# A recurrent loop's start-up moved among the last two column tiles of the projection before it

## The chip, the cores and the metric

The kernel runs on one core of a Trainium2 chip. One launch computes two transformer-like blocks in fp32; the time is the device time of one execution, in microseconds (us). A core has five engines that run their own instruction streams side by side and meet only at semaphores: TensorE (PE, matmuls), VectorE (DVE), ScalarE (ACT, activation functions), GpSimd (POOL) and SyncE (SP, which issues the transfers).

## The reference, cut to what matters

The second block mixes tokens in two ways; the part touched here is the RWKV mixer. 768 tokens (256 of context, 512 of the sequence) are projected to r, k, v and three small latents, each passed through a three-tap convolution over tokens. Then, for 8 heads of 64 and for two directions, a decay rate, a gain and a recurrence are computed:

```
parts = h @ p['w_in'];  rw = dwconv(parts[..., :RWKV_COLS], p['rwkv_conv'])
r, k, v, wl, al, gl = jnp.split(rw, RWKV_SPLITS, axis=-1)
kk = heads(k * p['k_k']);  kk = kk / jnp.maximum(norm(kk), 1e-12)
w_lat = jnp.tanh(wl)
for each direction:
    w = -softplus(-(w0 + w_lat @ w2)) - 0.5;  decay = exp(-exp(w))
    a = sigmoid(a0 + al @ a2)
    k_dir = k * (1.0 + (a - 1.0) * p['k_a'])
step: sa = einsum('bhvk,bhk->bhv', S, kk_t)
      S  = S * w_t - sa * b_t + v_t * k_t        # b = kk * a
      y  = einsum('bhvk,bhk->bhv', S, r_t)
```

## The kernel before, in words

The program is a list of phases. In a phase each engine has a function of its own, and `build` runs them in order; at the end of a phase every engine drains, raises its `phase_end` semaphore and waits until all the others have raised theirs (`boundary`, L615 on). If a phase is marked `soft`, TensorE alone doesn't wait there; it goes on into the next phase, and a call of `settle` (L516) later makes it wait for the other engines' `phase_end`.

**The projection** (`rwkv_projection`, L2469) works through 14 `items`: the two latent groups, then four column tiles each of k, r and v (`items[10]` to `items[13]` are the v tiles). For a k or v tile TensorE runs 8 matmuls of 256 columns (the context tokens) and 8 of 512 columns (the sequence), all by `block_feature` (L512), into one of three pairs of PSUM banks, `pair(n) = n % 3` (banks 0 to 5). ScalarE then copies both parts with the middle tap (L2594), and VectorE adds the two neighbour taps (L2619, L2621, twice each). `free` counts tiles that VectorE has finished, so it tells when a pair of banks may be written again. Banks 6 and 7 serve the norm of kk and the bonus term; the last to use them are the bonus sums of item 11 (L2572), copied out by ScalarE (L2614, counted by `bonus_copied`). `floored` counts the four normalised kk tiles (last written at L2657). ScalarE ends the phase by touching the sigmoid table with a one-element activation (L2615).

**The loop** (`rwkv_loop`, L2684) handles 12 chunks of 64 tokens in both directions. Two chunks make a block. For a block, in each direction `d`: `latents(b, d)` is one matmul of 512 columns and four of 128 on 33 rows (L2747, L2749) into banks 2 and 3; `rate(b, d)` is two sigmoids on ScalarE (L2942, L2943), to `SIG` and `RATE`; `cums(b, d)` sums the rates over tokens with 8 small matmuls (L2758; 16 in the profile, since an fp32 matmul is recorded as two) into banks 2 and 3; `exps(b, d)` is three activations with the exponential (L2950, L2951, L2954; a fourth in blocks of the sequence); `rate_products` and `key_products` are six VectorE operations (L3012, L3016, L3022) and `products(b, d)` three for a context block (L3030, L3034, L3036). For block 0 this is the loop's prologue: nothing overlaps it, and bank pair 2, 3 is written four times in turn. For later blocks the same helpers are called between the steps of earlier chunks.

The chunk loop then starts at n = -1 with `gram(0, B)` (L2680, 16 matmuls of a 64x64 tile, into bank 6), `latents(1, 0)`, `gram(0, K)` (L2673), `latents(1, 1)`, and from n = 0 on goes through five levels per chunk (`t_level`, `xy_level`: matmuls of 64x64 tiles, with copies on ScalarE at L2970 and, on VectorE, a subtraction at L3058 and a transposition at L3042 between them). At n = -1 VectorE's part is: mask gram B (L3047, `evacuate_b`), make Y (L3039, `y_init`), mask gram K (L3053), transpose (L3042). GpSimd adds the identity to Y (L3130, `eye`) and masks the level matrices (L3121); it has nothing to do in the projection. The order of the work is the order in which the code is written; there is no planner here.

`RW` places the loop's tiles in three areas of on-chip memory that are free once the loop runs: the projection's scratch (`R_TMP` on), its input (`A_A`), and the ring of weight tiles (`O_RING`), which the projection reads until its last matmul.

Of the kernel before, what the change touches and what calls it, by code (L numbers as in the profile page):

```python
# [20 lines left out]
P = 128  # L21
D = 1024
KD = D // P
S = 512
# [1995 lines left out]
for _n, _w in (("x1", 2 * CH), ("y1", 2 * CH), ("gram", 8 * CH), ("level", LEVELS * 2 * CH), ("eye", CH),  # L2020
# [8 lines left out]

RW = regions([(R_TMP, WORDS), (A_A, A_B), (O_RING, O_VEC)],  # L2030
             [("AR", 4096), ("X", 2048), ("B", 2048), ("K", 2048), ("GB", 2048), ("GK", 2048), ("LOFF", LEVELS * 512),
              ("SIG", 1024), ("RATE", 1024), ("VTK", 1024), ("S", 1024), ("T", 512), ("KTK", 512), ("BTK", 512), ("KV", 512),
              ("SA", 512)])
# [435 lines left out]
def rwkv_projection(k):  # L2469
# [60 lines left out]

    def tensor(k, pe):
        for n, (x, f) in enumerate(items):
            if n < 2:
                continue
            if n % 2 == 0:
                wt = k.pe_stream.take(KD, 256)
            if n >= 3:
                pe.wait_ge(free, n - 2)
            else:
                pe.wait_ge(k.attention["spread_read"], k.attention_count["spread_read"] + 2)  # L2540
            two = [k.bank[2 * pair(n)], k.bank[2 * pair(n) + 1]]
            _, _, m, c0 = part(n)
            if x in "kv":
                block_feature(pe, two[1][0:m, :NC_CTX], wt, c0, m, lambda q: C[:, q, :], KD)
            block_feature(pe, two[0][0:m, :], wt, c0, m, lambda q: A[:, q, :], KD).then_inc(k.half_done, 1)
            if n == 2:
                settle(k, pe, "diff_post")
            if x == "k":
                if f == 0:
                    pe.wait_ge(k.rwkv_in, 16 * N_RWKV_LOADS)  # L2550
                    pe.wait_ge(free, 1)
                else:
                    pe.wait_ge(gained, 2 * f)
                for d in range(2):
                    pe.matmul(k.bank[6 + d], W2A[64:97, d, f * P:(f + 1) * P], WA[64:97, NC_CTX:], start=True,
                              stop=True).then_inc(gains, 1)
            if x == "r":
                if f == 0:
                    pe.wait_ge(gained, 8)
                else:  # L2560
                    pe.wait_ge(rooted, f)
                pe.wait_ge(squared, f + 1)
                pe.matmul(k.bank[6], HEADSUM, SQ[:, f % 2, 0:512], start=True, stop=True)
                pe.matmul(k.bank[7][:, :256], HEADSUM, SQ[:, f % 2, 512:768], start=True, stop=True).then_inc(summed, 1)
            if x == "v" and f < 2:
                for g in (2 * f, 2 * f + 1):
                    pe.wait_ge(weighed, g + 1)
                    if f == 0:
                        pe.wait_ge(rooted, 4)
                    else:  # L2570
                        pe.wait_ge(bonus_copied, g - 1)
                    pe.matmul(k.bank[6 + g % 2], HEADSUM, BT[:, g, :], start=True, stop=True).then_inc(bonus_sum, 1)  # L2572

    def scalar(k, act):
        for n, (x, f) in enumerate(items):
            if x == "r":
# [40 lines left out]
    def vector(k, dve):  # L2617
        def neighbours(x, y, taps, cnt):
# [10 lines left out]
        for n, (x, f) in enumerate(items):  # L2629
            dve.wait_ge(centred, n + 1)  # L2630
# [28 lines left out]
    return Phase("rwkv_projection", sync=sync, tensor=tensor, vector=vector, scalar=scalar)  # L2659
# [24 lines left out]
def rwkv_loop(k):  # L2684
# [50 lines left out]

    halves = lambda n, lv, d: 2 * LEVELS * n + 2 * lv + d + 1
# [5 lines left out]
    def tensor(k, pe):  # L2742
        wait = lambda name, value: pe.wait_ge(sems[name], value)

        def latents(b, d):
            tok = block_tokens(b, d)
            pe.matmul(k.bank[2], WA[0:33, tok], W2A[0:33, d, :], start=True, stop=True)  # L2747
            for f in range(4):
                mm = pe.matmul(k.bank[3][:, f * P:(f + 1) * P], W2A[64:97, d, f * P:(f + 1) * P], WA[64:97, tok],  # L2749
# [3 lines left out]
        def cums(b, d):  # L2753
            wait("rated", prep(b, 1))
            sums = mask(k, "sums", 0, 256).rearrange("p (w c t) -> p w c t", w=2, c=2)
            for f in range(4):
                for c, rows in enumerate(HEADS):
                    mm = pe.matmul(k.bank[2 + c][:, f * P:(f + 1) * P], SIG[d][rows, f * P:(f + 1) * P], sums[rows, :, c, :],  # L2758
# [135 lines left out]
        pe.wait_ge(k.rwkv_in, 16 * N_RWKV_LOADS)  # L2894
        latents(0, 0)
        wait("rated", 1)
        latents(0, 1)
        wait("rated", 2)
        cums(0, 0)
        wait("exps", 1)  # L2900
        cums(0, 1)
        for n in range(-1, NCH + 1):
            m, g, live = n - 1, n + 1, 0 <= n < NCH
            for lv in range(LEVELS):
# [13 lines left out]
                if lv == 1:  # L2918
# [3 lines left out]
                    else:  # L2922
                        rest(aside)
                if lv in (3, 4) and rated_in(n) is not None:
                    prepare(n, lv - 3)
# [11 lines left out]
    def scalar(k, act):  # L2937
        wait = lambda name, value: act.wait_ge(sems[name], value)

        def rate(b, d):  # L2940
            wait("latent_done", prep(b, d))
            act.activation(SIG[d], k.bank[2], ACT.Sigmoid)  # L2942
            act.activation(RATE[d], k.bank[3], ACT.Sigmoid).then_inc(sems["rated"], 1)  # L2943

        def exps(b, d):
            wait("cums_done", prep(b, d))
            cum = k.psum[:, 1024:2048].rearrange("p (c f w t) -> p f w c t", c=2, f=4, w=2)
# [12 lines left out]
        for d in range(2):  # L2960
            rate(0, d)
        for d in range(2):
            exps(0, d)
        for n in range(-1, NCH + 1):
# [31 lines left out]
    def vector(k, dve):  # L2996
# [76 lines left out]
        dve.memset(ST[0], 0.0).then_inc(sems["state"], 1)  # L3073
        rate_products(0)
        key_products(0)
        for d in range(2):
            products(0, d)
        for n in range(-1, NCH + 1):
# [59 lines left out]
    return Phase("rwkv_loop", tensor=tensor, vector=vector, scalar=scalar, pool=pool)  # L3138
# [289 lines left out]
```

## Time and profile before

| | us |
|---|---|
| median of 3 runs | 2642.1 (2641.81 to 2643.7) |
| the profiled execution: its own time | 2645.46 |
| its span, from the first to the last instruction | 2643.7 |
| TensorE busy | 2487.0 (94% of the span) |
| VectorE, ScalarE, GpSimd busy | 1346.0, 513.4, 127.6 |
| projection's last two v tiles on TensorE | 1767.67 to 1788.32 |
| loop's prologue | 1788.32 to 1807.38 |
| chunk loop | 1807.38 to 2119.9 |

The span is one profiled execution. Instructions have a start and a duration; an engine's idle time is put down to the semaphore event that ended it. The chain of waits follows the work that ended last back from the end, so what lies on it sets the time. "PEclk" is the TensorE clock that was granted: 1.00 is 2.4 GHz and 0.50 is 1.2 GHz.

### The profile page before, as it was taken

How to read it: one execution, taken by the hardware profiler on the slowest of the kernel's cores; microseconds unless marked ns; L12 is line 12 of the kernel's file. 1: busy time of each engine (PE TensorE's matmuls, PEld its weight loads, DVE VectorE, ACT ScalarE, POOL GpSimd, SP SyncE). 2: the span in 40 equal slices, each digit the busy share in tenths (PEclk: the TensorE clock that was granted, in tenths of full speed). 3: DMA queues.
4: the chain of work that ended last, by engine and by line, in shares of the span. 5: the costliest groups of instructions: out<-in, count | busy, mean ns of one | idle time of the engine just before them, and what ended most of it. 6: DMA issues, size and time to landing. Idle time of an engine off the chain costs nothing.

```text
span 2643.7 us, 45304 instructions
## 1 busy us (share of the span) xinstructions
PE 2487.0 (94%) x19512; PEld 1932.5 (73%) x19512; DVE 1346.0 (51%) x2582; ACT 513.4 (19%) x1032; POOL 127.6 (5%) x106
## 2 busy tenths in 40 slices
PE   8989999999999999999998999997888898999997
PEld 5945888888586548888885664556788846888786
DVE  5625555533454426555432255465666536787533
ACT  2122100100003421000001034223434222212100
POOL 0000000000000000000000000002322200000000
PEclk9988999999999999999999989997999998999998
DMA  5323322233212014222234200300000033223232
GB/s 167 122 78 128 96 67 93 76 88 108 65 65 65 1 64 128 66 94 86 66 88 144 69 32 15 104 0 2 4 4 4 4 103 121 78 83 96 53 86 69
DMA packets 221166, 190.28 MB, mean 72 GB/s; under 512 B 8727, under 2 KB 219064, under 8 KB 220968
## 3 DMA queue, kind: packets, MB, share of 16 engines
q1 hardware_dynamic: 220674, 187.29, 22.9%
q8 instruction: 155, 2.54, 0.4%
q14 instruction: 43, 0.35, 0.0%
q10 hardware_dynamic: 294, 0.09, 0.0%
HBM read 185.25 MB, written 2.10 MB: 71 GB/s over the span
## 4 chain that ended last, share of the span: by engine, by line
PE 87%; DVE 6%; ACT 2%; issue 2%; SPq 1%; DMA 1%; POOL 1%; DVEq 0%; POOLq 0%; ACTq 0%
PE psum L1630 30%; PE psum L1840 14%; PE psum L512 8%; PE psum L2673 6%; PE psum L1130 4%; PE psum L1344 3%; PE psum L1341 3%; PE psum L3211 2%; PE psum L542 2%; PE psum L2680 1%; PE psum L1066 1%; PE psum L2252 1%; PE psum L2270 1%; PE psum L1109 1%; DVE sbuf L3042 1%
## 5 line engine op out<-in xcount | busy, mean ns | idle before, releaser
L1630 PE MATMUL psum<-sbuf 128*128 128x256 f32 x3696 | 804.5, 381 | 3.5 <-DVE sbuf L476 1.9
L1630 PEld LDWEIGHTS psum<-sbuf 128*128 128x128 f32 x3696 | 705.9, 191 | 101.7 <-issue 3.1
L1840 PE MATMUL psum<-sbuf 128*128 128x256 f32 x1848 | 405.2, 382 | 11.1 <-DVE sbuf L1858 5.5
L1840 PEld LDWEIGHTS psum<-sbuf 128*128 128x128 f32 x1848 | 353.8, 192 | 62.1 <-DVE sbuf L1858 6.3
L1714 DVE TENSOR_TENSOR sbuf<-sbuf,psum 128x256 f32<-128x256 f32 x462 | 177.8, 417 | 200.0 <-PE psum L1630 198.7
L512 PE MATMUL psum<-sbuf 128*128 128x512 f32 (+3 forms) x688 | 247.9, 519 | 4.3 <-DVEq L617 4.0
L2673 PE MATMUL psum<-sbuf 64*64 64x64 f32 (+1 forms) x5952 | 209.6, 223 | 32.4 <-DVE sbuf L3058 10.1
L2673 PEld LDWEIGHTS psum<-sbuf 64*64 64x64 f32 x5952 | 194.8, 136 | 44.5 <-issue 24.5
L512 PEld LDWEIGHTS psum<-sbuf 128*128 128x128 f32 (+2 forms) x688 | 129.4, 189 | 115.5 <-issue 103.4
L1876 DVE TENSOR_TENSOR sbuf<-sbuf,psum 128x256 f32<-128x256 f32 x84 | 34.2, 419 | 231.6 <-PE psum L1840 231.2
L427 POOL TENSOR_TENSOR sbuf<-sbuf 128x512 f32<-128x512 f32 x30 | 37.8, 1279 | 1923.1 <-DVE sbuf L413 1922.9
L1130 PE MATMUL psum<-sbuf 128*128 128x512 f32 x256 | 117.0, 607 | 0.0
L1650 ACT ACTIVATE sbuf<-sbuf 128x512 f32<-128x512 f32 x44 | 27.7, 630 | 399.7 <-DVE sbuf L1714 399.7
L3121 POOL TENSOR_TENSOR sbuf<-sbuf 128x512 f32<-128x512 f32 x60 | 75.0, 1273 | 576.1 <-DVE sbuf L3047 545.7
L1130 PEld LDWEIGHTS psum<-sbuf 128*128 128x128 f32 x256 | 48.1, 195 | 53.1 <-issue 53.1
L1700 DVE TENSOR_TENSOR sbuf<-sbuf 128x512 f32<-128x512 f32 x66 | 44.5, 690 | 81.1 <-PE psum L1630 67.1
L1344 PE MATMUL psum<-sbuf 128*128 128x256 f32 x392 | 85.4, 379 | 0.0
L1344 PEld LDWEIGHTS psum<-sbuf 128*128 128x128 f32 x392 | 74.2, 190 | 11.3 <-issue 1.3
L1178 DVE TENSOR_REDUCE sbuf<-psum 128x1 f32<-128x256 f32 (+3 forms) x80 | 36.8, 460 | 89.1 <-PE psum L1066 51.7
L3058 DVE TENSOR_TENSOR sbuf<-sbuf,psum 128x256 f32<-128x256 f32 x120 | 47.6, 403 | 66.5 <-PE psum L2673 66.1
L1341 PEld LDWEIGHTS psum<-sbuf 128*128 128x128 f32 x672 | 75.4, 192 | 0.1
L1341 PE MATMUL psum<-sbuf 128*128 128x128 f32 x672 | 75.4, 275 | 0.0
(281 smaller groups left out, 2687.9 us busy)
## 6 DMA issues: line engine op xcount, KB each, us to landing
sbuf<-in_w_mod_dram SPq DMA_DIRECT2D x24, 1024.0 KB, 5.1
sbuf<-in_w_ffn_gate_dram SPq DMA_DIRECT2D x22, 1024.0 KB, 5.5
sbuf<-in_w_ffn_up_dram SPq DMA_DIRECT2D x22, 1024.0 KB, 8.0
sbuf<-in_w_ffn_down_dram SPq DMA_DIRECT2D x32, 704.0 KB, 6.0
sbuf<-in_w_up_dram SPq DMA_DIRECT2D x22, 1024.0 KB, 7.2
sbuf<-in_w_out_dram SPq DMA_DIRECT2D x12, 1024.0 KB, 7.7
sbuf<-in_w_in_dram SPq DMA_DIRECT2D x12, 1024.0 KB, 5.5
sbuf<-in_w_down_dram SPq DMA_DIRECT2D x16, 704.0 KB, 5.8
```

Source lines behind the costliest of these rows:

```text
L512: mm = pe.matmul(bank, w[:, q, c0:c0 + m], rhs(k0 + q), start=start and q == 0, stop=stop and q == kc - 1)
L542: mm = pe.matmul(bank, act_chunk(q), w[:, q, :], start=q == 0, stop=q == kc - 1)
L1130: mm = pe.matmul(bank_of(b), tiles[b // 2][:, q, (b % 2) * P:(b % 2) * P + P], MIX[:, q, :], start=q == 0, stop=q == KD - 1)
L1341: mm = pe.matmul(self.bank(p)[:, t * P:(t + 1) * P], x[:, q, t * P:(t + 1) * P], w[:, q, :], start=q == 0, stop=q == 3)
L1344: mm = pe.matmul(self.bank(p), w[:, q, :], x[:, q, :], start=q == 0, stop=q == 3)
L1630: mm = pe.matmul(bank, w[:, q, :], rhs[:, q, :], start=q == 0, stop=q == 3)
L1714: dve.tensor_tensor(out, base, bank_of(u, p, t), ALU.add).then_inc(s["added"], 1)
L1840: mm = pe.matmul(bank_of(g, p), wt[:, q, :], rhs_of[p][:, q, :], start=q == 0, stop=q == UNITS - 1)
L2673: mm = pe.matmul(out[h], lhsT[h], rhs[h], start=start, stop=stop)
L3058: dve.tensor_tensor(y, y, k.bank[d][:, 256:512], ALU.subtract).then_inc(sems["xy"], 1)
L3121: pool.tensor_tensor(split(LOFF[lv]), split(GB[g % 2][:, :, 0, :]), both_level(lv), ALU.mult).then_inc(sems["loff"], 1)
L3211: mm = pe.matmul(block_bank(b), tiles[b // 2][:, q, (b % 2) * P:(b % 2 + 1) * P], MIX[:, q, :], start=q == order(b)[0], stop=q == order(b) ...
```

## The change

Each engine's function of the loop becomes a generator (`tensor_steps`, `scalar_steps`, `vector_steps`) with `yield` between the parts of the prologue. The projection's functions start these generators and take their steps at set places among items 12 and 13; the loop's own phase runs what remains. The prologue's banks for block 0 come from `home`: 6 and 7 for direction 0, 4 and 5 for direction 1. The projection is marked soft, and TensorE settles after `gram(0, B)`, before `latents(1, 0)`. Loop tiles that block 0 writes this early are placed elsewhere (`RW_RING`).

```diff
+RW_RING = [("RATE", 1024), ("B", 2048), ("LOFF", LEVELS * 512), ("K", 2048), ("VTK", 1024), ("S", 1024), ("T", 512), ("KTK", 512), ("BTK", 512), ("KV", 512), ("SA", 512)]
...
+    def begin(k, name, eng):
+        steps = k.rwkv_steps[name] = k.rwkv_steps[name](k, eng)
+        next(steps)
+        return steps
     def tensor(k, pe):
+        steps = begin(k, "tensor", pe)
...
+            if n == 13:
+                pe.wait_ge(free, 12)
+                next(steps)
             if x in "kv":
                 block_feature(pe, two[1][0:m, :NC_CTX], wt, c0, m, lambda q: C[:, q, :], KD)
+            if n == 12:
+                pe.wait_ge(bonus_copied, 4)
+                next(steps)
+            if n == 13:
+                next(steps)
             block_feature(pe, two[0][0:m, :], wt, c0, m, lambda q: A[:, q, :], KD).then_inc(k.half_done, 1)
...
     def scalar(k, act):
+        steps = begin(k, "scalar", act)
         for n, (x, f) in enumerate(items):
+            if n == 12:
+                act.activation(k.M[0:1, O_SML + 205:O_SML + 206], k.eps[0:1, :], ACT.Sigmoid)
+                next(steps)
+            if n == 13:
+                act.wait_ge(floored, 4)
+                next(steps)
...
     def vector(k, dve):
+        steps = begin(k, "vector", dve)
...
         for n, (x, f) in enumerate(items):
+            if n == 13:
+                dve.wait_ge(floored, 4)
+                next(steps)
             dve.wait_ge(centred, n + 1)
...
-    return Phase("rwkv_projection", sync=sync, tensor=tensor, vector=vector, scalar=scalar)
+    ph = Phase("rwkv_projection", sync=sync, tensor=tensor, vector=vector, scalar=scalar)
+    ph.soft = True
+    return ph
...
+    home = lambda b, d: 2 if b else (6, 4)[d]
...
-    def tensor(k, pe):
+    def tensor_steps(k, pe):
...
-        pe.wait_ge(k.rwkv_in, 16 * N_RWKV_LOADS)
+        yield
         latents(0, 0)
-        wait("rated", 1)
+        yield
         latents(0, 1)
-        wait("rated", 2)
-        cums(0, 0)
-        wait("exps", 1)
-        cums(0, 1)
+        yield
+        for d in range(2):
+            cums(0, d)
+        yield
         for n in range(-1, NCH + 1):
...
+                if n == -1 and lv == 3:
+                    settle(k, pe, "rwkv_projection")
                 if lv in (3, 4) and rated_in(n) is not None:
                     prepare(n, lv - 3)
...
-    def scalar(k, act):
+    def scalar_steps(k, act):
...
-        for d in range(2):
-            rate(0, d)
+        yield
+        rate(0, 0)
+        yield
+        rate(0, 1)
         for d in range(2):
             exps(0, d)
+        yield
...
-    def vector(k, dve):
+    def vector_steps(k, dve):
...
-        dve.memset(ST[0], 0.0).then_inc(sems["state"], 1)
+        yield
         rate_products(0)
         key_products(0)
         for d in range(2):
             products(0, d)
+        yield
+        dve.memset(ST[0], 0.0).then_inc(sems["state"], 1)
         for n in range(-1, NCH + 1):
```

On TensorE, before the change, items 11 to 13 are followed by the prologue and by gram B (L512 is the projection, L2747 and L2749 the latents, L2758 the sums, L2680 gram B, L2673 gram K):

```order
L2572 MATMUL psum<-sbuf 128x512 x2
L512 MATMUL psum<-sbuf 128x256 x8
L512 MATMUL psum<-sbuf 128x512 x8
L512 MATMUL psum<-sbuf 128x256 x8
L512 MATMUL psum<-sbuf 128x512 x8
L2747 MATMUL psum<-sbuf 128x512
L2749 MATMUL psum<-sbuf 128x128 x4
L2747 MATMUL psum<-sbuf 128x512
L2749 MATMUL psum<-sbuf 128x128 x4
L2758 MATMUL psum<-sbuf 128x128 x16
L2680 MATMUL psum<-sbuf 64x64 x16
```

And with the change, in the same stretch of TensorE (the latents are now L2775 and L2777, the sums L2786, gram B L2707):

```order
L2585 MATMUL psum<-sbuf 128x512 x2
L512 MATMUL psum<-sbuf 128x256 x8
L2775 MATMUL psum<-sbuf 128x512
L2777 MATMUL psum<-sbuf 128x128 x4
L512 MATMUL psum<-sbuf 128x512 x8
L2775 MATMUL psum<-sbuf 128x512
L2777 MATMUL psum<-sbuf 128x128 x4
L512 MATMUL psum<-sbuf 128x256 x8
L2786 MATMUL psum<-sbuf 128x128 x16
L512 MATMUL psum<-sbuf 128x512 x8
L2707 MATMUL psum<-sbuf 64x64 x16
```

The latents stand before the sequence part of item 12 and before the context part of item 13; both directions' sums stand between the two parts of item 13; gram B follows the last projection matmul directly.

On VectorE, with the change, this stands around items 12 and 13 (L2641 and L2643 are the neighbour taps, L3046 to L3070 the prologue's products, L3113 the clearing of the state, L3081 the masking of gram B):

```order
L2643 SCALAR_TENSOR_TENSOR sbuf<-psum,sbuf 128x255
L3046 SCALAR_TENSOR_TENSOR sbuf<-sbuf 128x512 x2
L3050 TENSOR_TENSOR sbuf<-sbuf 128x512 x2
L3056 SCALAR_TENSOR_TENSOR sbuf<-sbuf 128x512 x2
L3064 TENSOR_TENSOR sbuf<-sbuf 128x8x64
L3068 TENSOR_TENSOR sbuf<-sbuf 128x512
L3070 TENSOR_TENSOR sbuf<-sbuf 128x512
L3064 TENSOR_TENSOR sbuf<-sbuf 128x8x64
L3068 TENSOR_TENSOR sbuf<-sbuf 128x512
L3070 TENSOR_TENSOR sbuf<-sbuf 128x512
L2641 SCALAR_TENSOR_TENSOR sbuf<-psum,sbuf 128x511
L2643 SCALAR_TENSOR_TENSOR sbuf<-psum,sbuf 128x511
```

All twelve product operations now stand between the taps of item 12 and the taps of item 13; before, they stood after item 13's taps and the clearing of the state.

On ScalarE the same stretch, with the change (L2614 is the middle tap, L2972 and L2973 the rates, L2981 to L2985 the exponentials):

```order
L2973 ACTIVATE sbuf<-psum 128x512
L2981 ACT_TABLE_LOAD
L2981 ACTIVATE sbuf<-psum 128x8x64
L2982 ACTIVATE sbuf<-psum 128x512
L2985 ACTIVATE sbuf<-psum 128x8
L2981 ACTIVATE sbuf<-psum 128x8x64
L2982 ACTIVATE sbuf<-psum 128x512
L2985 ACTIVATE sbuf<-psum 128x8
L2614 ACTIVATE sbuf<-psum,sbuf 128x512
L2614 ACTIVATE sbuf<-psum,sbuf 128x256
L2635 ACT_TABLE_LOAD
L2635 ACTIVATE sbuf<-sbuf 1x1
```

The rates and exponentials of block 0 now stand ahead of item 13's middle tap, and the load of the sigmoid table, three loads in all as before, is the last thing of the phase.

## Rows read from the trace of the kernel before

**Rows 1.** The page: granted clock in 40 slices of the span, and the chain by engine.
```profile
PEclk9988999999999999999999989997999998999998
...
PE 87%; DVE 6%; ACT 2%; issue 2%; SPq 1%; DMA 1%; POOL 1%; DVEq 0%; POOLq 0%; ACTq 0%
```

**Rows 2.** Chain of waits, 1735 to 1835 us: start, us on the chain, engine and line.
```profile
1767.67 20.65 PE psum L512 x64
...
1798.67 2.10 PE psum L2758 x16
...
1807.38 1.97 PE psum L2680 x32
...
1811.36 1.90 PE psum L2673 x32
...
1815.27 2.78 PE psum L2673 x48
...
1823.16 0.68 PE psum L2673 x16
...
1826.10 0.33 PE psum L2673 x4
...
1828.64 1.09 PE psum L2758 x16
```

**Rows 3.** Busy time by stage: stretch, length, PE, PEld, DVE, ACT, POOL, PEclk, DMA, GB/s.
```profile
1767.67:1788.32 20.65, 20.64 (x64) 11.81 (x63) 4.15 (x8) 1.65 (x3) 0.00 (x0) 1.00 0.00 1
1788.32:1807.38 19.06, 8.22 (x52) 7.07 (x52) 10.62 (x17) 9.59 (x16) 0.00 (x0) 0.60 0.00 0
1792.12:1819.40 27.28, 19.85 (x206) 17.86 (x208) 12.23 (x23) 9.90 (x18) 7.40 (x6) 0.50 0.00 1
1819.40:2119.90 300.50, 259.18 (x8688) 244.78 (x8685) 183.06 (x396) 115.28 (x247) 82.22 (x66) 1.00 0.02 4
```

**Rows 4.** Chain of waits, 1850 to 1865 us: latents of a later block.
```profile
1854.57 0.31 PE psum L2747
...
1855.66 0.64 PE psum L2673 x16
```

**Rows 5.** Timeline, all engines, 1788 to 1813 us: start, us, engine, line; in brackets idle before.
```profile
1788.35 1.05 ACT L2594 ACTIVATE sbuf<-psum,sbuf 128x512 f32<-128x512 f32 x2 [9.27 <-PE psum L512]
1789.42 1.28 ACT L2615 ACT_TABLE_LOAD   x1
1790.71 0.20 ACT L2615 ACTIVATE sbuf<-sbuf 1x1 f32<-1x1 f32 x1
...
1791.98 1.11 PE L2747 MATMUL psum<-sbuf 33*128 33x512 f32 x1 [3.67 <-DVEq L617]
...
1792.25 0.48 DVE L3073 MEMSET sbuf<- 128x512 f32 x1 [0.37 <-issue]
...
1797.44 0.60 ACT L2942 ACTIVATE sbuf<-psum 128x512 f32<-128x512 f32 x1 [2.23 <-PE psum L2749]
...
1800.37 1.29 DVE L3022 SCALAR_TENSOR_TENSOR sbuf<-sbuf 128x512 f32<-128x512 f32 x2
...
1805.31 0.69 DVE L3030 TENSOR_TENSOR sbuf<-sbuf 128x512 f32<-128x512 f32 x1 [1.31 <-ACT sbuf L2954]
...
1809.40 0.69 DVE L3047 TENSOR_TENSOR sbuf<-psum,sbuf 128x512 f32<-128x512 f32 x1 [2.08 <-PE psum L2680]
1810.01 0.68 DVE L3039 TENSOR_TENSOR sbuf<-psum,sbuf 128x512 f32<-128x512 f32 x1
1811.49 1.27 POOL L3130 TENSOR_TENSOR sbuf<-sbuf 128x512 f32<-128x512 f32 x1
```

**Rows 6.** Timeline of PE at two places: an earlier phase, and the second level.
```profile
903.91 1.25 PE L1094 MATMUL psum<-sbuf 128*128 128x128 f32 x8 [2.16 <-ACT sbuf L1245]
...
1819.12 1.44 PE L2673 MATMUL psum<-sbuf 64*64 64x64 f32 x32 [0.24 <-DVE sbuf L3042]
```

**Rows 7.** Busy time just behind the first row of rows 6; columns as in rows 3.
```profile
905.00:908.00 3.00, 3.00 (x5) 0.97 (x4) 0.80 (x2) 0.18 (x1) 0.00 (x0) 0.50 0.00 0
```

More of the change, by code:

```diff
@@ L2027 @@
 assert R_G2 + 512 <= A_MIX
+RW_RING = [("RATE", 1024), ("B", 2048), ("LOFF", LEVELS * 512), ("K", 2048), ("VTK", 1024), ("S", 1024), ("T", 512), ("KTK", 512), ("BTK", 512), ("KV", 512), ("SA", 512)]
 RW = regions([(R_TMP, WORDS), (A_A, A_B), (O_RING, O_VEC)],
-             [("AR", 4096), ("X", 2048), ("B", 2048), ("K", 2048), ("GB", 2048), ("GK", 2048), ("LOFF", LEVELS * 512),
-              ("SIG", 1024), ("RATE", 1024), ("VTK", 1024), ("S", 1024), ("T", 512), ("KTK", 512), ("BTK", 512), ("KV", 512),
-              ("SA", 512)])
+             [("AR", 4096), ("X", 2048), ("GB", 2048), ("GK", 2048), ("SIG", 1024)] + RW_RING)
 MOD_DERIVED = ("gx", "gc", "gf", "pm", "pf")
@@ L2746, in latents @@
             tok = block_tokens(b, d)
-            pe.matmul(k.bank[2], WA[0:33, tok], W2A[0:33, d, :], start=True, stop=True)
+            pe.matmul(k.bank[home(b, d)], WA[0:33, tok], W2A[0:33, d, :], start=True, stop=True)
             for f in range(4):
-                mm = pe.matmul(k.bank[3][:, f * P:(f + 1) * P], W2A[64:97, d, f * P:(f + 1) * P], WA[64:97, tok],
+                mm = pe.matmul(k.bank[home(b, d) + 1][:, f * P:(f + 1) * P], W2A[64:97, d, f * P:(f + 1) * P], WA[64:97, tok],
                                start=True, stop=True)
@@ L2757, in cums @@
                 for c, rows in enumerate(HEADS):
-                    mm = pe.matmul(k.bank[2 + c][:, f * P:(f + 1) * P], SIG[d][rows, f * P:(f + 1) * P], sums[rows, :, c, :],
+                    mm = pe.matmul(k.bank[home(b, d) + c][:, f * P:(f + 1) * P], SIG[d][rows, f * P:(f + 1) * P], sums[rows, :, c, :],
                                    start=True, stop=True)
@@ L2941, in rate @@
             wait("latent_done", prep(b, d))
-            act.activation(SIG[d], k.bank[2], ACT.Sigmoid)
-            act.activation(RATE[d], k.bank[3], ACT.Sigmoid).then_inc(sems["rated"], 1)
+            act.activation(SIG[d], k.bank[home(b, d)], ACT.Sigmoid)
+            act.activation(RATE[d], k.bank[home(b, d) + 1], ACT.Sigmoid).then_inc(sems["rated"], 1)
         def exps(b, d):
             wait("cums_done", prep(b, d))
-            cum = k.psum[:, 1024:2048].rearrange("p (c f w t) -> p f w c t", c=2, f=4, w=2)
+            o = 512 * home(b, d)
+            cum = k.psum[:, o:o + 1024].rearrange("p (c f w t) -> p f w c t", c=2, f=4, w=2)
             incl, excl = cum[:, :, 0], cum[:, :, 1]
@@ L3136, in pool, with remaining, steps @@
                     loff(g, lv)
-    return Phase("rwkv_loop", tensor=tensor, vector=vector, scalar=scalar, pool=pool)
+    k.rwkv_steps = {"tensor": tensor_steps, "scalar": scalar_steps, "vector": vector_steps}
+    def remaining(name):
+        def steps(k, eng):
+            for _ in k.rwkv_steps[name]:
+                pass
+        return steps
+    return Phase("rwkv_loop", tensor=remaining("tensor"), vector=remaining("vector"), scalar=remaining("scalar"), pool=pool)
 def mixer_output(k, w, post):
```

## The prediction

> **What bounds the kernel now.** I read the page first: TensorE is the chain for 87% of the span, and its granted clock is near full everywhere but in some slices, the lowest of them (7 tenths) being the one that holds the start of the chunk loop [rows 1]. Then the table by stage. Over the last two v tiles TensorE is busy for 20.64 of 20.65 us at a clock of 1.00; in the prologue it is busy for 8.22 of 19.06 us, VectorE for 10.62 and ScalarE for 9.59, and none of these shares is near one: the stage is a relay in which each engine waits for the one before [rows 3]. The chain of waits says the same: TensorE is done with the projection at 1788.32 (1767.67 + 20.65), and gram B begins at 1807.38 [rows 2]. These 19.06 us are what the change can touch. The clock falls in them: from 1792.12 to 1819.40 it is 0.50, that is 1.2 instead of 2.4 GHz, and in the rest of the loop 1.00 [rows 3].
>
> **The work that TensorE takes into the projection.** Latents for two directions and sums for two directions. At full clock one direction's latents take 1.09 us (from 1854.57 to the next piece at 1855.66) [rows 4], and one direction's sums 1.09 us, against 2.10 in the prologue at half clock [rows 2]. Among the tiles TensorE has the full clock [rows 3], so the price is 4 x 1.09 = 4.36 us, and the last projection matmul ends at 1788.32 + 4.36 = 1792.68. Bounds: 4.36 at full clock; at half clock about 8.4.
>
> **Is everything in time among the tiles?** An item takes 20.65 / 2 = 10.32 us, a third of it (3.44) for the context columns, the rest 6.88. So latents 0 run at 1771.11 to 1772.20, and ScalarE, which is idle there (1.65 us busy in the whole stretch [rows 3]), has the table and both sigmoids done long before the sequence part ends at 1779.1. Latents 1 run to 1780.2. ScalarE's queue holds item 12's taps first (1.05 us, to 1780.2) and then the rates (two of 0.60 us, to 1781.4) [rows 5]; the exponential's table, 1.28 us, follows, to 1782.7. TensorE's context part ends at 1783.6, so the sums, which wait for the second rate, find it done 2.2 us before. They run to 1784.7 and 1785.8; the exponentials of direction 1 are done about 1787.1. VectorE finishes item 12's taps about 1782.7, then six rate and key products at 1.2 to 1.3 us for each two [rows 5], to 1786.3, and three products for each direction at about 2.05 us (the last three began at 1805.31 and gram B at 1807.38, rows 5 and 2), to 1790.4. Gram B needs them at 1792.68. The cover is 2.3 us. If it were gone, every us beyond it would be one on the path, but only on the way to gram B, which itself is not late before the tail below ends; the true slack is larger.
>
> **What is late next: the tail of item 13.** Its taps can't move. Before, the other engines were past the phase's end, and TensorE with them, at 1791.98, 3.66 us after the last matmul, and VectorE's clearing of the state began at 1792.25, 3.93 us after it [rows 5]. With the soft boundary TensorE runs gram B in that time for nothing, at about 1 us. VectorE's clearing then starts at 1792.68 + 3.93 = 1796.61 and, 0.48 us later, the masking of gram B at 1797.09. Before it began at 1809.40 [rows 5]: 12.3 us earlier. The new wait, settle, stands before latents 1, 0 on TensorE; behind it are gram K and all levels. It ends at 1792.68 + 3.66 = 1796.34; the latents take 1.09 us at full clock or 2.00 at half (between gram B's end, 1809.35, and 1811.36 [rows 2]), so at most to 1798.35. Y is ready 1.29 us after the masking begins (1810.01 + 0.68 - 1809.40 [rows 5]): 1798.38. So gram K starts at about 1798.4 in either case, where it started at 1811.36 [rows 2]: **12.96 us earlier**.
>
> A page of the Trainium skill speaks against this tail: ScalarE: Activation LUTs, section What ACT_TABLE_LOAD costs, gives about 2.66 us for every switch of table, a load of 1283 ns and a drain of about 1380 ns. The trace has the load at 1.28 us, and the activation behind it starts at 1790.71, at once [rows 5]; no drain is seen. With the page's drain ScalarE would end its phase at about 1792.3 instead of 1790.9, in the times of before, 0.3 us after the 1791.98 at which the phase ended, and the gain would be 12.6 instead of 12.96; I go by the row.
>
> **From gram K on: two levels of clock.** After gram B TensorE is idle from about 1793.7 to 1796.34, 2.6 us, then has 1 or 2 us of latents on 33 rows, an idle stretch of up to 1 us, gram K, and latents again. In an earlier phase an idle time of 2.16 us, ended at 903.91, was followed by a clock of 0.50 from 905 on [rows 6, 7]. In the loop the clock holds at 1.00 [rows 3]. I take it that the clock falls again. Then gram K (1.90), the latents behind it and the first level go as before: level 0 begins 3.91 us after gram K (1815.27 - 1811.36 [rows 2]) and level 1 3.85 us after that (1819.12 [rows 6]). The clock came back 4.1 us after level 0 began (1819.40 [rows 3]); if it now comes a few us later, that costs up to 0.9. If the clock doesn't fall, gram K takes 1 us less, but level 0 then waits for GpSimd's identity, done 3.36 us after the masking (1811.49 + 1.27 - 1809.40 [rows 5]), at 1800.45, and a transposition: it begins near 1801.0, 14.3 us earlier than before, and a level takes 2.94 us (1826.10 - 1823.16 [rows 2]) instead of 3.85: together 15.2 us earlier.
>
> **Further edits.** The new places of tiles, the generators and the banks of block 0 add no instruction but one table touch, under ScalarE's idle time. No transfer moves: SP's next loads wait for the loop's end, before and after. What follows level 1 is the same chain in the same order, so I count it at nothing; where a later pause makes the clock fall a little sooner or later, 1 or 2 us either way.
>
> **The sum.** -12.96, and 0.1 for the later return of the clock: -12.9. Against the profiled execution's own time, 2645.46, that is 2632.6; this execution is 3.4 above the median of the runs shown, 2642.1, and against that it is **2629.2**.
>
> **Rival A: the clock never falls.** For it: the idle time falls from over 10 us in pieces to one of 2.6. Against it: 2.16 us have sufficed elsewhere. Gain 15.2: 2626.9.
>
> **Rival B: a wait inside the projection.** TensorE takes up to three hand-overs among the tiles (bonus copies, the freed bank pair, the rates), each of which my times cover with 1 to 3 us. If one of the in-order queues is later than I think, or if the masking waits for VectorE longer than the tail, 3 to 5 us come back; in the prologue at half clock this work took about 8.4 us of TensorE instead of 4.36, a loss of the same size. Gain 8 to 10: about 2633. Against it: the work on ScalarE and VectorE in this stretch was 1.65 and 4.15 of 20.65 us [rows 3], so even with the prologue's shares neither is full.
>
> **Rival C, slower: the half clock stays in the loop.** The gap now lies right before the loop, whose levels are bursts of 64x64 matmuls with pauses. If these did not lift the clock, each level would cost 3.85 instead of 2.94 us, 0.91 more. The gain of 12.9 is used up after 14 levels, close to three of the 12 chunks; through half of the 60 levels it would be 27.3 - 12.9 = 14 us slower, 2656, and through all of them 42, 2684. Against it: the same levels lifted it before, within 4.1 us of their start.
>
> **Rival D: nothing changes**, 2642.1, if the soft boundary only moved the relay. It would take item 13's tail to be as long as the prologue; it is 3.93 of 19.06 us.
>
> **How the numbers follow.** The forecast with the clock fallen 0.56, A 0.20, B 0.16, C 0.04, D 0.04. A run of this kernel can tell 0.2%, 5.3 us, from no change. Forecast, A and B lie beyond it on the fast side, together 0.92; with the part of D and C that ends near zero: faster 0.93, same 0.04, slower 0.03. The range takes A with 1.5 us for a clock that falls differently elsewhere, 2625.4, and B's upper middle, 2634.2; what is outside is B's worst, C and D, and part of A, under 0.2.
>
> **What the new profile would show.** Right: the two v tiles' stretch on TensorE without a pause, 4.4 us longer, at a clock of 1.00; latents and sums at 1.09 us each; twelve products on VectorE before item 13's taps; gram B directly behind the last projection matmul; then one wait of about 2.6 us on TensorE, ended by VectorE; from the projection's old end to the masking of gram B 8.8 us instead of 21.1. A low clock that begins three to seven us after gram B and ends within the first two levels. Wrong: a pause on TensorE before the sums, or before gram B for the products (rival B); a clock of 1.00 throughout (A); a slice of the loop at half clock (C); a chunk loop, from gram B's masking on, longer than before by more than 1 us.

## The result and the profile after

The changed kernel takes 2629.85 us (median of 6 runs, 2625.46 to 2633.36), the kernel before 2641.95 on the same chip (6 runs, 2636.23 to 2643.7). The medians lie 12.1 us apart, where 12.9 and a time of 2629.2 had been forecast. The ratio on record, with its 95% interval, is 0.9947 (0.9932 to 0.9963). It isn't the quotient of the two medians, which is 0.9954; it stands for 14.0 us, and its interval for 9.8 to 18.0, so the change is faster beyond the noise and its size is known to a few us only. The profiled execution of the changed kernel took 2627.17 us with a span of 2625.4, and that of before had 2645.46 and 2643.7. So the two profiles lie 18.3 us apart and the medians 12.1. Both numbers have to be explained.

The page, as in [rows 1]: the slice that holds the start of the loop no longer stands out.

```profile
PEclk9988999999999999999999989999999998999998
```

The chain of waits of the changed kernel, which answers to [rows 2]: start, us on the chain, engine and line.

```profile
1767.86 3.45 PE psum L512 x16
...
1772.40 7.06 PE psum L512 x16
...
1780.56 3.65 PE psum L512 x16
1784.21 1.99 PE psum L2786 x32
1786.19 7.08 PE psum L512 x16
...
1793.30 0.69 ACT sbuf L2614
...
1797.19 0.48 DVE sbuf L3113
...
1798.87 1.97 PE psum L2700 x32
...
1802.85 2.78 PE psum L2700 x48
...
1806.70 1.81 PE psum L2700 x32
...
1810.99 0.68 PE psum L2700 x16
```

Busy time by stage as in [rows 3], in the same columns: the last two v tiles, the tail, the stretch at half clock, and the rest of the loop.

```profile
1767.67:1792.68 25.01, 25.01 (x117) 15.55 (x115) 11.73 (x20) 8.84 (x17) 0.00 (x0) 1.00 0.00 1
1792.60:1797.00 4.40, 1.88 (x36) 1.10 (x34) 2.37 (x4) 2.54 (x4) 0.00 (x0) 1.00 0.00 0
1797.95:1808.19 10.24, 9.22 (x137) 8.58 (x136) 4.77 (x12) 3.19 (x7) 7.42 (x6) 0.50 0.01 2
...
1813.00:2107.00 294.00, 258.71 (x8558) 242.18 (x8557) 179.66 (x391) 117.38 (x249) 82.17 (x66) 1.00 0.03 9
```

TensorE is busy through the whole of the two tiles (25.01 of 25.01 us), also with the prologue's work in it, and VectorE and ScalarE do theirs beside it (11.73 and 8.84 us, where [rows 3] had 4.15 and 1.65). The relay of 19.06 us has shrunk to the tail of item 13. The stretch at half clock is 10.24 us long instead of 27.28.

The timelines of ScalarE, VectorE and TensorE over the same place, which answer to [rows 5].

```profile
1781.79 1.28 ACT L2981 ACT_TABLE_LOAD   x1
1785.35 0.60 ACT L2981 ACTIVATE sbuf<-psum 128x512 f32<-128x512 f32 x1 [2.28 <-PE psum L2786]
...
1794.36 1.28 ACT L2635 ACT_TABLE_LOAD   x1
1795.66 0.20 ACT L2635 ACTIVATE sbuf<-sbuf 1x1 f32<-1x1 f32 x1
```

```profile
1789.81 0.69 DVE L3070 TENSOR_TENSOR sbuf<-sbuf 128x512 f32<-128x512 f32 x1
1794.38 0.75 DVE L2641 SCALAR_TENSOR_TENSOR sbuf<-psum,sbuf 128x511 f32<-128x511 f32 x1 [3.88 <-ACT sbuf L2614]
...
1797.60 0.63 DVE L3081 TENSOR_TENSOR sbuf<-psum,sbuf 128x512 f32<-128x512 f32 x1
```

```profile
1793.36 1.15 PE L2707 MATMUL psum<-sbuf 64*64 64x64 f32 x32
1796.92 0.69 PE L2775 MATMUL psum<-sbuf 33*128 33x512 f32 x1 [2.41 <-DVEq L617]
...
1798.87 1.97 PE L2700 MATMUL psum<-sbuf 64*64 64x64 f32 x32 [0.78 <-DVE sbuf L3073]
```

All twelve products end at 1790.50, and gram B stands directly behind the last projection matmul. TensorE's long wait behind it, 2.41 us, is ended by the phase's end; a short one of 0.78 us stands before gram K.

**Where the 18.3 us of the two profiles lie.** At the second level (1806.70 against 1819.12 [rows 6]) the changed kernel is 12.42 us ahead. The next phase begins at 2119.92 before and at 2101.28 after, 18.64 us apart; so another 6.22 us lie inside the chunk loop, whose code the change leaves as it is (what follows the loop gives 0.3 back). Three chains of waits, at the first matmuls of that phase: before, the changed kernel, and the changed kernel in a second profiled execution (the run "again" below).

```profile
2119.92 2.84 PE psum L3179 x6
```

```profile
2101.28 2.84 PE psum L3223 x6
```

```profile
2112.12 2.84 PE psum L3223 x6
```

From the second level to this row it is 300.80 us before, 294.58 in the first profile of the changed kernel, and 303.95 (from 1808.17) in its second. The same program differs from itself by 9.4 us there. The chains show where: in pieces of "issue", such as these of the changed kernel's first profile, and in the run "again" in two further spells at half clock.

```profile
1847.00 1.30 issue
...
1918.10 1.41 issue
```

Over this stretch "issue" has 6.2% of the chain before (18.6 us), 4.7% in the first profile of the changed kernel (13.8) and 6.1% in its second (18.5): 4.8 of the 6.22 us, and 4.7 of the 9.4. The profiles of the other runs below have 295 to 300 us for the same stretch (fill 296.9, hard 297.4, head 300.4, head_fill 295.2, twice 297.8, products_back 295.8, rates_only 299.6), in no order that follows their edits. So I count the 12.4 us that stand at the second level as the change's, and the 6.2 us behind it as chance of one execution. The medians (12.1) agree; their interval is too wide to exclude a small effect inside the loop.

### The profile page after: what moved, and what is told of

Same layout as the page of the kernel before. It is cut to its first block, busy times and chain, and to the rows that moved or that the text cites. A ratio compares the mean times of both kernels' runs of the same rounds, so it can differ in the third digit from the quotient of the medians.

```text
span 2625.4 us, 45306 instructions
## 1 busy us (share of the span) xinstructions
PE 2481.6 (95%) x19512; PEld 1930.4 (74%) x19512; DVE 1344.9 (51%) x2582; ACT 513.1 (20%) x1033; POOL 127.6 (5%) x106
## 4 chain that ended last, share of the span: by engine, by line
PE 87%; DVE 6%; ACT 2%; issue 1%; SPq 1%; POOL 1%; DMA 1%; DVEq 0%; POOLq 0%; ACTq 0%
PE psum L1630 31%; PE psum L1840 15%; PE psum L512 8%; PE psum L2700 6%; PE psum L1130 4%; PE psum L1344 3%; PE psum L1341 3%; PE psum L3255 2%; PE psum L542 2%; PE psum L1066 1%; PE psum L2251 1%; PE psum L2707 1%; PE psum L2269 1%; PE psum L1109 1%; PE psum L325 1%
## 5 line engine op out<-in xcount | busy, mean ns | idle before, releaser
L512 PE MATMUL psum<-sbuf 128*128 128x512 f32 (+3 forms) x688 | 250.0, 522 | 4.3 <-DVEq L617 4.0
L512 PEld LDWEIGHTS psum<-sbuf 128*128 128x128 f32 (+2 forms) x688 | 130.4, 191 | 115.6 <-issue 103.0
```

Of the source, the lines that this page charges most:

```text
L512: mm = pe.matmul(bank, w[:, q, c0:c0 + m], rhs(k0 + q), start=start and q == 0, stop=stop and q == kc - 1)
```

## The experiments

Whole times of single executions scatter by several us, so each run is read by landmarks, counted from the start of item 12's context columns (the row of 3.45 us on L512): the end of the last projection matmul, the masking of gram B on VectorE, and the start of the second level. Before they stand at 20.65, 41.73 and 51.45 us; in the changed kernel at 25.41, 29.74 and 38.84.

**twice: what the moved matmuls cost.** Every latents group and every sums group of block 0 among the tiles is issued two times; the first copy is overwritten.

```diff
+        latents(0, 0, False)
         latents(0, 0)
...
+        latents(0, 1, False)
         latents(0, 1)
...
+            cums(0, d, False)
             cums(0, d)
```

> The changed kernel with the moved latents and sums of block 0 issued twice on TensorE (the first copy signals nobody). Theory (what TensorE takes in among the tiles is paid one to one, everything else hides behind it): in the changed kernel the doubled pieces took 1.10, 1.09 and 1.99 us, so the end of the projection, the masking of gram B and the first level all come 4.2 us later than in the changed kernel, and nothing else moves; VectorE's products still end before the last projection matmul. Rival (TensorE has room in this stretch and the relay of the other engines sets the end): the masking comes less than 1 us later. Rival (the products are just in time): more than 5 us later, with a pause on TensorE before gram B.

One run, 2629.6 us. The second copies make the stretch 3.58 us longer (28.99 instead of 25.41), and the masking comes 3.57 us later, where 4.2 had been expected. TensorE's timeline of this kernel:

```profile
1768.79 0.69 PE L2775 MATMUL psum<-sbuf 33*128 33x512 f32 x1
...
1769.75 0.59 PE L2775 MATMUL psum<-sbuf 33*128 33x512 f32 x1
...
1783.47 3.84 PE L2787 MATMUL psum<-sbuf 64*128 64x128 f32 x64
1787.25 7.13 PE L512 MATMUL psum<-sbuf 128*128 128x512 f32 x16
1794.49 1.15 PE L2707 MATMUL psum<-sbuf 64*64 64x64 f32 x32
```

The second copy of one direction's latents costs 0.9 us, where the first takes 1.10, and the second copies of the sums 1.8, where the first take 1.99: what repeats a shape is cheaper by 0.2. The work added in the projection comes out at the masking in full, though gram B still finds the products done (they end at 1790.7, gram B starts at 1794.49): it is TensorE that sets the end of this stretch.

**products_back: what the products are worth.** The twelve products of VectorE go back behind the phase's end, and the rest of the prologue stays among the tiles. TensorE settles before gram B, and no longer behind it.

```diff
@@ tensor_steps, before gram B
+        settle(k, pe, "rwkv_projection")
@@ vector_steps: the yield that ended block 0's products stands ahead of them
+        yield
...
-        yield
```

> The changed kernel with only VectorE's twelve products of block 0 put back behind the phase's end; latents, rates, sums and exponentials stay among the tiles. Theory (the gain is the length of a relay, of which VectorE's products are the longest leg, and they can't start before item 13's taps and the boundary): products begin at about 17.2 on the clock on which the changed kernel clears the state at 1797.2, take 12 x 0.62 = 7.4 us, then gram B at half clock 1.97, so the masking comes about 9.3 us later than in the changed kernel and 3 of the 12.4 us of gain are left: the time is 2638 to 2640. Rival (what was saved is mostly TensorE's own 8.2 us at half clock, now run in 4.2): the masking comes only 3 to 5 us later and the time is 2633 to 2635.

2639.37 us (10 runs), against 2641.77 of before, measured beside it (13 runs), ratio 0.9989, 0.9976 to 1.0003: no gain that can be told from none. All engines of this kernel, around its gram B:

```profile
1796.67 1.29 DVE L3045 SCALAR_TENSOR_TENSOR sbuf<-sbuf 128x512 f32<-128x512 f32 x2 [0.66 <-issue]
...
1803.54 0.69 DVE L3069 TENSOR_TENSOR sbuf<-sbuf 128x512 f32<-128x512 f32 x1
...
1804.38 1.97 PE L2707 MATMUL psum<-sbuf 64*64 64x64 f32 x32 [12.00 <-DVE sbuf L3069]
...
1806.39 0.69 DVE L3080 TENSOR_TENSOR sbuf<-psum,sbuf 128x512 f32<-128x512 f32 x1 [1.61 <-PE psum L2707]
```

TensorE waits 12.00 us for the last product. The masking is at 39.42, 9.68 us later than in the changed kernel, of which 7.56 are the products (1796.67 to 1804.23) and 2.16 gram B, which is now on the path and at half clock (1804.23 to 1806.39). Of the 12.0 us that the changed kernel gains at the masking, 2.3 are left, near the 3 expected; the rival, 3 to 5 us later, is refuted.

**rates_only: the first half alone.** Only the latents and the rates stay among the tiles; sums, exponentials and products stand behind the phase's end, and the last touch of the sigmoid's table is dropped. TensorE settles before the sums.

```diff
@@ tensor_steps, before the sums
+        settle(k, pe, "rwkv_projection")
@@ scalar_steps, vector_steps: yields moved ahead of exponentials and products
@@ scalar, behind item 13's taps
-        act.activation(k.M[0:1, O_SML + 205:O_SML + 206], k.eps[0:1, :], ACT.Sigmoid)
```

> The changed kernel with only latents and rates of block 0 among the tiles; sums, exponentials and products stand behind the phase's end, TensorE waits there ahead of the sums. Theory (TensorE's pieces cost their full time among the tiles, and pay only if what they release is also moved; the relay behind the boundary is set by VectorE's twelve products): from item 12's context columns the last projection matmul ends after 23.1 us, 2.2 earlier than with the sums among the tiles; products start at 27.5 and end near 35, gram B's masking comes at 37.1, that is 7.4 us later than in the changed kernel but 2.3 us EARLIER than with sums and exponentials moved and products not (39.4). Rival (each moved part gains by itself): the masking comes later than 39.4.

One run, 2639.0 us. Its chain at the place, from all engines' timeline:

```profile
1795.11 3.67 PE L2783 MATMUL psum<-sbuf 64*128 64x128 f32 x32 [3.74 <-DVEq L617]
...
1803.78 1.97 PE L2704 MATMUL psum<-sbuf 64*64 64x64 f32 x32 [5.01 <-DVE sbuf L3065]
...
1805.80 0.69 DVE L3076 TENSOR_TENSOR sbuf<-psum,sbuf 128x512 f32<-128x512 f32 x1 [1.53 <-PE psum L2704]
```

The masking is at 37.6, 1.8 us **earlier** than with the sums moved as well (39.42). The products take 8.1 us on VectorE behind the boundary (1795.67 to 1803.73) instead of 7.6. The sums and exponentials run beside the rate products there and cost only this 0.5 us, most of it a wait of 0.41 us for the exponentials; moved, they make TensorE's stretch 2.17 us longer (25.41 against 23.24). This gives the change in steps at the masking: latents and rates -4.1, sums and exponentials +1.8, products -9.7, together -12.0. The middle step alone is a loss at this landmark, read from one execution of each kernel; it pays because the products can't move without it.

**hard: the boundary alone.** The soft boundary and its settle are taken away, so every engine waits for the phase's end before gram B.

```diff
-    ph.soft = True
...
-                if n == -1 and lv == 3:
-                    settle(k, pe, "rwkv_projection")
```

> The changed kernel without the soft boundary: TensorE waits at the end of the projection for the other engines, and the later wait is gone. Theory (gram B's own 1 us was all that the soft boundary hid, the tail is VectorE's): gram B starts at the end of the tail, 3.65 us after the last projection matmul, and takes 1.1 us at full clock or 2.0 at half, so the masking comes 0.5 to 1.3 us later than in the changed kernel, and the first level 0.5 to 2 us later. Rival (the soft boundary carries a large share of the gain): the masking comes more than 2.5 us later.

One run, 2636.51 us. In this execution item 12 began only at 1775.04, 7.2 us later than in the changed kernel, in code that is the same, so its whole time says nothing here. The landmarks do (timeline of all engines):

```profile
1804.12 1.15 PE L2706 MATMUL psum<-sbuf 64*64 64x64 f32 x32 [3.67 <-DVEq L617]
...
1805.31 0.69 DVE L3078 TENSOR_TENSOR sbuf<-psum,sbuf 128x512 f32<-128x512 f32 x1 [0.44 <-PE psum L2706]
```

The masking is at 30.27, 0.53 us later, and the second level at 39.18, 0.34 later. The soft boundary hides gram B, but VectorE's clearing of the state, 0.48 us, lies beside it anyway: it is worth 0.3 to 0.5 us of the 12.

**fill: what the half clock costs.** Matmuls whose results nothing reads fill TensorE's waits: 1280 columns behind gram B and 384 before gram K (2.41 and 0.91 us in the profile).

```diff
+                    for f in range(2):
+                        pe.matmul(k.bank[7], k.ident, src["K"][:, f, 0:512], start=True, stop=True)
+                    pe.matmul(k.bank[7][:, 0:256], k.ident, src["K"][:, 2, 0:256], start=True, stop=True)
...
+                    prepare(n, 0)
+                    pe.matmul(k.bank[7][:, 0:384], k.ident, src["K"][:, 3, 0:384], start=True, stop=True)
```

> The changed kernel with four extra matmuls that compute nothing that is used: 512, 512 and 256 columns of fp32 into bank 7 between gram B and the wait for the phase's end, 384 columns after the latents of block 1, direction 0. Theory (the clock fell at 1797.95 because TensorE was idle for 2.4 us and then had little to do): the clock stays at 1.00 through the start of the loop; gram K starts where it did, takes 1.1 instead of 1.97 us, the first level starts 1.4 us earlier (then GpSimd's identity is late next) and the second one 2.3 to 2.5 us earlier; time 2627 to 2628. Rival (the clock falls for the loop's small matmuls themselves): clock 0.50 all the same and no gain, or a loss of up to 1 us from the fillers. Rival (the fillers delay the latents): the same or slower by 0.3.

2625.27 us (4 runs, 2623.92 to 2627.41), where 2627 to 2628 had been expected, against 2641.77, ratio 0.9929, 0.9912 to 0.9945. The granted clock is 1.00 through the loop's start. TensorE's timeline of this kernel:

```profile
1797.83 1.15 PE L2700 MATMUL psum<-sbuf 64*64 64x64 f32 x32
...
1800.48 2.30 PE L2700 MATMUL psum<-sbuf 64*64 64x64 f32 x64 [0.41 <-DVE sbuf L3081]
1803.41 1.38 PE L2700 MATMUL psum<-sbuf 64*64 64x64 f32 x32 [0.63 <-DVE sbuf L3081]
...
1808.07 2.13 PE L2700 MATMUL psum<-sbuf 64*64 64x64 f32 x50 [1.42 <-DVE sbuf L3081]
```

Gram K takes 1.15 us instead of 1.97. The masking is where it was (29.75), the second level at 36.60, 2.24 us earlier. At the third level 1.87 us are left (41.26 against 43.13): TensorE now waits 1.42 us for VectorE, whose rate products of the next block stand ahead of the transposition. So the half clock in the changed kernel costs it 1.9 to 2.2 us at these landmarks. That is near rival A's price as the prediction had it, 15.2 - 12.9 = 2.3. The medians would give fill 4.4 us over the changed kernel (2625.27 against 2629.85, which were not measured side by side); no row shows the rest.

**again: the changed kernel once more**, unchanged, measured side by side with head and head_fill below.

> The changed kernel itself, on the chip and in the call of the three kernels beside it, for a fair comparison with them. Both theories: 2627 to 2632; measured from the start of item 12's context columns, the masking of gram B 29.7 us later and the second level 38.8 us later, give or take 0.5 for when the clock returns; what differs between two profiled executions lies elsewhere.

2632.59 us (4 runs, 2630.64 to 2634.47) against 2645.02 of before beside it, ratio 0.9954, 0.9939 to 0.9969; 2627 to 2632 had been expected. The second level is at 38.6, 0.2 us from the first profile's. What differs is the loop (303.95 us, above), with two spells in it that the first profile lacks, this one and one of about the same length from 1944:

```profile
1889.60:1893.00 3.40, 3.40 (x49) 3.40 (x46) 0.27 (x1) 0.39 (x1) 3.40 (x4) 0.50 0.02 5
```

**head: more of the prologue inside.** Gram B goes before the last two of the eight matmuls of item 13's sequence columns; the maskings, the initial Y, gram K's transpositions and GpSimd's mask and identity come before the phase's end, and the second block's latents use banks that are free earlier.

```diff
+            if n == 13:
+                block_feature(pe, two[0][0:m, :], wt, c0, m, lambda q: A[:, q, :], 6, stop=False)
+                next(steps)
+                block_feature(pe, two[0][0:m, :], wt[:, 6:8, :], c0, m, lambda q: A[:, q, :], 2, k0=6, start=False).then_inc(k.half_done, 1)
...
+        rest(gram(0, B, "gram_b"))
+        yield
+        rest(gram(0, K, "gram_k"))
+        wait("exps", 2)
+        latents(1, 0)
+        pe.wait_ge(k.rwkv_bank_free, 14)
+        latents(1, 1)
...
+    latent_home = lambda b, d: 4 if (b, d) == (1, 0) else home(b, d)
```

> The changed kernel, going further: gram B of chunk 0 stands before the last two of item 13's eight sequence matmuls; VectorE masks it and makes Y before item 13's taps, and masks gram K and transposes before the phase's end; GpSimd's first level mask and its identity run in the projection too; gram K follows the last projection matmul; latents of block 1 use banks 4, 5 for direction 0, and banks 2, 3 for direction 1 as soon as item 13's taps are done; TensorE settles before the second level. Theory (after the change the tail of item 13 on ScalarE and VectorE, 3.5 us, and what VectorE does after it are the bound, so all that needs not wait for it belongs before it): from item 12's context columns the first level starts after 31.5 us, where it was 34.9, and the second after 34.5 to 35.5, where it was 38.8; time 2625 to 2627. Rival (gram B inside the last tile only lengthens the tail by its own 1.15 us and by the switch between matmul shapes): the second level starts at 38 to 40, no gain.

2625.32 us (4 runs, 2624.14 to 2629.6), ratio 0.9932, 0.9915 to 0.9949. All engines of this kernel, from gram B to the second level:

```profile
1789.51 1.15 PE L2718 MATMUL psum<-sbuf 64*64 64x64 f32 x32
...
1790.70 0.69 DVE L3100 TENSOR_TENSOR sbuf<-psum,sbuf 128x512 f32<-128x512 f32 x1 [1.62 <-PE psum L2718]
...
1796.19 0.69 PE L2787 MATMUL psum<-sbuf 33*128 33x512 f32 x1 [1.28 <-DVE sbuf L2649]
...
1797.30 1.97 PE L2711 MATMUL psum<-sbuf 64*64 64x64 f32 x32
...
1797.61 0.60 ACT L2991 ACTIVATE sbuf<-psum 128x512 f32<-128x512 f32 x1 [2.43 <-DVEq L617]
...
1800.00 1.97 PE L2711 MATMUL psum<-sbuf 64*64 64x64 f32 x32 [0.73 <-ACT sbuf L3023]
...
1802.31 1.92 PE L2711 MATMUL psum<-sbuf 64*64 64x64 f32 x32 [0.34 <-DVE sbuf L3095]
```

The first level begins at 31.4 as expected, 3.5 us earlier than in the changed kernel (34.9), but the second at 36.4 where 34.5 to 35.5 had been expected. ScalarE is held at the phase's end until 1797.61, then has four rates in its queue (2 us) before the copy that the second half of level 0 waits for. The relay was moved ahead of the boundary, and ScalarE's queue was not.

The clock also fell in this kernel, behind an idle time of only 1.28 us:

```profile
1797.40:1804.02 6.62, 5.55 (x96) 5.21 (x98) 2.76 (x7) 3.00 (x7) 4.94 (x4) 0.50 0.00 1
```

**head_fill: the same with the clock held up**, by three more matmuls of 256 columns that nothing reads (six in the profile, 1.49 us).

```diff
+        for f in range(3):
+            pe.matmul(k.bank[0][:, 0:256], k.ident, src["K"][:, f, 0:256], start=True, stop=True)
```

> As the kernel with the loop's head moved too, with three extra matmuls of 256 columns into bank 0 (nothing uses them) in TensorE's remaining idle time before item 13's taps are done. Theory (2 us and more of idle time make the clock fall): the kernel without fillers idles some 1.4 us there and keeps 1.00 or nearly, so the fillers bring 0 to 1 us; if it falls without them, they hold it and the second level starts 34.5 us after item 12's context columns. Rival (fillers delay the first level): later by 0.3 us or more than without.

2624.95 us (4 runs, 2623.85 to 2629.03), ratio 0.9928, 0.9913 to 0.9943. The clock is 1.00 through the loop's start, the levels take less, and the wait for ScalarE grows from 0.73 to 1.42 us (TensorE's timeline of this kernel):

```profile
1803.03 1.15 PE L2711 MATMUL psum<-sbuf 64*64 64x64 f32 x32 [1.42 <-ACT sbuf L3025]
```

The second level is at 36.0, where 34.5 had been expected and head has 36.4, and the third at 40.0 instead of 40.8. The theory of this run is refuted in its main point: without the fillers the clock did not keep 1.00, it was 0.50 from 1797.4 to 1804.0 in head, behind 1.28 us of idle time. The two remedies overlap: together they give 2.9 and 3.1 us over the changed kernel at these two levels, where each alone gives 1.9 to 2.4. fill, head and head_fill, at 2625.27, 2625.32 and 2624.95, are all below both kernels by the median, and can't be told from one another; fill is the smallest edit of the three. Against again, measured beside them, head and head_fill are 7.3 and 7.6 us faster by the median, more than the 2.3 to 3.1 that the landmarks show; the rest isn't explained by any row.

## Why the prediction was right, by its own steps

**TensorE's share in the projection** was mis-sized: 4.36 us forecast, 4.76 measured (25.41 - 20.65). Latents (1.10 for each direction) and sums (1.99 for both) together are 4.19, even less than forecast. The rest are the neighbours: a sequence part takes 7.06 and 7.08 us where a third of 20.65 gives 6.88 (an item's two thirds), and the context part behind latents 3.65 instead of 3.45. All three stand directly behind a small group, so what changed was the shape that precedes them (33 or 64 rows instead of 128; a change from 256 to 512 columns at 128 rows costs nothing in these rows). The run twice fits: it repeats the three small groups without a new change of shape, and adds 3.58 us and not the 4.19 that they take, 0.2 less for each. So the groups themselves are worth 3.58, and six changes of shape, into and out of three groups, at 0.2 make up the 4.76. Two more runs agree: in rates_only the whole of item 13's matmuls behind latents takes 10.53 us for 10.32, and in head the sequence part that gram B splits takes 5.35 + 1.93 = 7.28 us for 6.88, 0.2 for each entry. Why a change of shape costs this stays open.

**The cover** was 2.3 us forecast, 2.86 measured (products done at 1790.50, gram B at 1793.36), and no wait arose among the tiles. The sums of both directions ran in one go, as forecast, and the exponentials were done at about 1787.6, where 1787.1 had been forecast. Rival B is refuted. What the cover is worth, products_back shows: with the products behind the boundary the masking comes 9.7 us later.

**The tail** was forecast at 3.66 and 3.93 us and measured at 3.65 and 3.92. The Trainium skill (ScalarE: Activation LUTs, What ACT_TABLE_LOAD costs) gives about 2.66 us for a switch of table, about 1380 ns of them a drain. This case's trace doesn't agree: the load takes 1.28 us, from 1794.36, where item 13's taps end on ScalarE, to 1795.64, and the activation begins at 1795.66, so no drain is seen on either side. The gain of 12.6 that the prediction worked out with the drain lies near the measured 12.4 by chance; the tail itself was as long as without it.

**The masking** came at 1797.60 (forecast 1797.09) and gram K at 1798.87 (1798.4), 12.49 us earlier than before instead of 12.96. The difference is the 0.40 of the first step, and 0.19 by which item 12 began later in this execution, less 0.1 from shorter steps on VectorE.

**The clock** fell, as forecast: from 3.4 us after gram B's end, to 1.5 us into the second level. Level 0 began 3.98 us after gram K and level 1 3.85 after that, as before, and the third level kept 12.17 us, so the later return cost 0.25, not 0.1. Rival A is a real possibility, only not the one that this kernel takes by itself: fill puts its price at 1.9 to 2.2 us. The prediction held against it that 2.16 us of idle time had sufficed elsewhere; in head even 1.28 us sufficed. Rival C is refuted: the levels lift the clock as they did before, and it is 1.00 from 1813 to 2107. Short spells such as that of 1889.60 to 1893.00 occur in some executions (two in again, one each in head, twice and rates_only, none in the loops of the other six profiles); at half clock for 3.40 us one costs at most 1.7. Rival D is refuted by the masking, 12 us earlier.

**The sum** was 12.9; the landmarks give 12.4 at the second level and 12.2 at the third, the medians 12.1 here and 12.4 beside again. So the mechanism was right, and of the sum's terms TensorE's share was mis-sized, by 0.40 us, and the clock's return, by 0.15. That the median came within 0.7 us of the forecast is partly luck: single runs of the changed kernel lie between 2625.46 and 2633.36, and the ratio's interval is 8 us wide. The step from the profiled execution (2645.46) to the median of before, 3.4 us, was right to be made: that execution was slower than all six runs of before. Where it lost the 3.4 us isn't shown; its loop, 300.80 us, is within what the other profiles have, 294.6 to 304.0. Without the second profile of the changed kernel the 6.2 us in the loop would have looked like a gain of the change.

What isn't settled is what the "issue" pieces are. They come in executions of all kernels here, at differing places; no run was made to tell.

## What to carry to other kernels

A prologue that is a relay of several engines belongs beside a stage in which one engine is full: it then costs that engine's own part, here 4.8 us paid for 16.8 us of path taken away (12.0 gained at the masking and the 4.8), and not the relay's length. But move the whole chain up to the engine that releases the next stage, since a part of it alone can lose (sums and exponentials without the products: +1.8 us), and look what stands in each in-order queue behind the boundary. Read a gain of this size at landmarks counted from a common start, over two profiles, before any difference far from the edit is explained.

## What the runs showed of the hardware

- Where TensorE's fp32 stream changed between matmuls of 128 rows and of 33 or 64, about 0.2 us went each time (7.06 for 6.88, 3.65 for 3.45, and 1.10 against 0.9 for latents first and repeated).
- TensorE idle for 2.41 us, then busy for 9.22 of 10.24 us with 33-row and 64x64 matmuls, was at half clock for these 10.24; 2.4 us of 128-row matmuls in the wait (1793.40 to 1795.81 in fill) and 0.9 before gram K kept it at 1.00, with the same small matmuls behind them. An idle time of 1.28 us (head, to 1796.19) was also followed by 0.50, from 1797.4 to 1804.0.
- The same program's loop, some 8,600 matmuls as the profile counts them, took 294.6 and 304.0 us in two executions; of the 9.4 us, 4.7 are pieces of "issue", and at most 3.4 two spells at half clock.
